# Three 256-token output projections recast as seven products of quarters, with tokens on the output partitions

## The chip, the cores and the metric

The kernel runs on one core of one Trainium2 chip. A core has a matrix engine (TensorE, PE in the profile), a vector engine (VectorE, DVE), a scalar engine (ScalarE, ACT), GpSimd (POOL), and DMA queues, here mostly issued from SyncE (SP). All arithmetic is 32-bit floating point. The metric is the device time of one launch, in microseconds (us); lower is better.

## The reference, cut to what matters

The reference runs a two-stream block of depth 2 and then a second block of depth 2, model width 1024. In every mixer the attention-like parts are concatenated into 1024 features per token, multiplied by a 1024x1024 output matrix, normalised over the features of a token and added to the residual stream:

```python
D_MODEL = 1024; SEQ = 256; NORM_EPS = 1e-6
def rms_norm(x, g):
    y = x * lax.rsqrt(jnp.mean(x * x, -1, keepdims=True) + NORM_EPS)
    return y * g
# first block, layer 1 (the "odd" mixer), latent tokens only:
y_lat = jnp.concatenate([c_lat.reshape(b, s_len, -1), d_lat.reshape(b, s_len, -1)], -1) @ w_out
# second block, for both layers (the "sparse" mixer):
mix = jnp.concatenate([y_attn, y_conv, y_pool], axis=-1)
mix = jnp.einsum('bse,ed->bsd', mix, w_out[i])
h = h + rmsnorm(mix, norm_mix_post[i])
m = rmsnorm(h, norm_mlp_pre[i])
m = jnp.square(jax.nn.relu(jnp.einsum('bsd,df->bsf', m, w_up[i])))
```

These are three products of 256 tokens x 1024 by 1024 x 1024: one in the odd mixer, one in each of the two sparse mixers. A fourth output projection, of the even mixer, has 512 tokens and is not part of the change.

## The kernel before, in words

Activations are kept with features on the 128 partitions: a tensor of 1024 features is eight tiles (k = 0 to 7) of 128 partitions by 256 or 512 tokens. `h` ("residual" in the profile) is the residual stream, `u` ("normed") the normalised input of a product, `y` ("branch") a product's output. The mixer's output lies in `R.mixed` (in "arena") for the odd mixer and in `R.mix2` ("mix") for the sparse ones.

Weights are read as 128x128 blocks, 16 to a chunk of 1 MB. SyncE loads all chunks in the order of use into a ring of five slots ("weight_ring"); a slot is loaded again when the last product that uses its chunk is done (`K.next_blocks` records which).

The program is a list of stages. Each stage adds a piece of program for each engine, and every engine runs its pieces strictly in the order of the stages (`K.add`); semaphores with counted values order the engines against each other. There is no scheduler. `K.in_turn` makes each vector instruction wait for the one before it where they depend on each other.

Around each of the three projections the stages are:

- `attention_stage` (L709): scores, softmax, transposed probabilities (L763), weighted values (L784). Its last instruction is on VectorE, L840, which writes the last part of the mixer's output. What the other mixers' parts wrote is there earlier.
- `matmul_stage` (L355, product at L396) with `squares=True`: for each of eight output tiles m, eight matmuls, with a weight block as the stationary operand and 128x256 activations as the moving one, into one of four banks of PSUM. ScalarE copies each result to `y` and squares it (L384); VectorE adds up the squares (L378). `root_table` (L530) loads ScalarE's table for the square root ahead of it.
- `residual` (L565) with `token_norm` (L497): the sum over the partitions by a matmul with ones (L513), root (L508), reciprocal (L522), and the spreading of the token's factor over partitions by a matmul (L517); then for each tile two instructions on VectorE, `y*gain*factor` (L575) and `h + y` (L581).
- `modulated_norm` (L535) with `scale_stage` (L446): ScalarE squares each tile of `h` as it is ready (L464), with two buffers for the squares; TensorE sums them by matmuls with ones (L482), eight accumulated in one bank; then the root (L469), a reciprocal of 128x256 (L490) and a scaling per tile (L546), of which the next product starts with the first tile. In the odd stage ScalarE also adds a shift (L558).
- the first product of the feed-forward part: L892 after the odd mixer, L396 from "normed" after the sparse ones.

`WideFeedForward` (L914), an older part of the kernel for 512 tokens, already uses seven products of quarters; its vector instructions on weights (L951 to L954) have the size of those that the change adds.

## Time and profile before

| | us |
|---|---|
| median of 3 runs | 2405.7 |
| lowest, highest | 2405.43, 2406.46 |
| the profiled execution, its own time | 2402.14 |
| its span, from the first to the last instruction | 2400.3 |
| TensorE busy in the span | 2271.0 (95%) |
| VectorE, ScalarE, GpSimd busy | 814.5, 462.9, 104.1 |
| granted TensorE clock, mean | 0.971 of full speed |

The page of the profile says which share of the span each engine is busy, which chain of instructions ended last, and which groups of instructions cost most. In rows of a group "L396 PE MATMUL out<-in 128*128 128x256 f32 x1504 | 325.6, 379" the figures behind the bar are the busy time of the group in us and the mean duration of one instruction in ns. One matmul of 32-bit data appears as two records of TensorE, and matmuls are pipelined: the mean duration of one is longer than the distance from one to the next, so a run's cost is its busy time over its records. PEld is the load of the stationary operand, which overlaps the matmuls. The granted clock is given as a share of full speed: 1.00 is 2.4 GHz, 0.50 is 1.2 GHz.

### The profile page before, as it was taken

The page shows a single profiled execution, that of the slowest core. Times are in us where ns is not written, and L with a number is a line of the kernel's source. Part 1 is how long each engine was busy: PE and PEld are TensorE (multiplying, and loading weights), DVE is VectorE, ACT ScalarE, POOL GpSimd, SP SyncE. Part 2 cuts the span into 40 slices and gives each one's busy share as a digit, 9 for nine tenths or more (in the row PEclk, how much of TensorE's full clock was granted, in tenths as well). Part 3 has the DMA queues.
Part 4 walks back from the last instruction along what each step waited for, and adds up shares of the span by engine and source line. Part 5 has one row for each costly group of instructions (what it writes and reads, how often), then busy time and mean ns, then how long its engine had stood idle before and what let it go on. Part 6 is the DMA issues. An engine that isn't in the chain of part 4 may idle for free.

```text
span 2400.3 us, 34069 instructions
## 1 busy us (share of the span) xinstructions
PE 2271.0 (95%) x15078; PEld 1713.8 (71%) x15078; DVE 814.5 (34%) x1541; ACT 462.9 (19%) x999; POOL 104.1 (4%) x126
## 2 busy tenths in 40 slices
PE   6999999998999999979999999988999999889998
PEld 3447877453888864454678888876888878678887
DVE  1565545643544440032331001763110138421002
ACT  2433221442100000020431000133110012311001
POOL 0003332001100000000000000000000000000000
PEclk8999999999999999989999999999999999899999
DMA  7221444205422222121123444322343333134332
GB/s 309 70 70 57 162 158 163 94 19 185 130 89 86 85 76 70 70 84 57 53 71 123 158 140 158 114 88 71 129 152 140 143 131 113 66 111 157 123 146 99
DMA packets 39074, 271.30 MB, mean 113 GB/s; under 512 B 4752, under 2 KB 6160, under 8 KB 6928
## 3 DMA queue, kind: packets, MB, share of 16 engines
q1 hardware_dynamic: 36752, 261.11, 30.6%
q0 software_dynamic: 1312, 3.15, 0.7%
q10 hardware_dynamic: 864, 4.87, 0.5%
q8 instruction: 119, 1.95, 0.3%
q14 instruction: 27, 0.22, 0.0%
HBM read 267.54 MB, written 1.05 MB: 112 GB/s over the span
## 4 chain that ended last, share of the span: by engine, by line
PE 87%; DVE 8%; ACT 3%; DMA 1%; issue 1%; ACTq 0%; DVEq 0%
PE banks L396 39%; PE banks L980 11%; PE banks L892 6%; PE banks L1472 5%; PE banks L2119 4%; PE banks L1155 2%; PE banks L1179 2%; PE banks L434 2%; PE banks L608 1%; PE banks L748 1%; PE banks L1175 1%; DVE arena L2271 1%; PE banks L482 1%; PE banks L763 1%; PE banks L754 1%
## 5 line engine op out<-in xcount | busy, mean ns | idle before, releaser
L396 PE MATMUL banks<-arena,weight_ring 128*128 128x256 f32 (+1 forms) x1856 | 476.8, 420 | 1.7 <-ACT arena L2534 0.9
L396 PEld LDWEIGHTS banks<-arena,weight_ring 128*128 128x128 f32 x1856 | 352.4, 190 | 125.2 <-issue 83.5
L396 PE MATMUL banks<-normed,weight_ring 128*128 128x256 f32 (+1 forms) x1296 | 305.3, 399 | 12.9 <-DVE normed L546 11.8
L396 PEld LDWEIGHTS banks<-normed,weight_ring 128*128 128x128 f32 x1296 | 250.0, 193 | 68.5 <-issue 19.1
L378 DVE TENSOR_TENSOR roots<-roots,squares 128x256 f32<-128x256 f32 (+1 forms) x56 | 27.6, 492 | 555.6 <-ACT squares L384 555.6
L892 PE MATMUL banks<-normed,weight_ring 128*128 128x256 f32 x704 | 152.2, 379 | 3.4 <-ACT normed L558 3.4
L2119 PE MATMUL banks<-normed,weight_ring 128*128 128x256 f32 x640 | 147.3, 391 | 5.9 <-DVE normed L546 5.9
L892 PEld LDWEIGHTS banks<-normed,weight_ring 128*128 128x128 f32 x704 | 133.6, 190 | 22.0 <-ACT normed L558 3.8
L2119 PEld LDWEIGHTS banks<-normed,weight_ring 128*128 128x128 f32 x640 | 125.1, 196 | 25.9 <-issue 4.7
L1472 PE MATMUL banks<-normed,weight_ring 128*128 128x512 f32 x288 | 126.1, 593 | 0.0
L396 PE MATMUL banks<-mix,weight_ring 128*128 128x256 f32 (+1 forms) x384 | 111.0, 451 | 3.0 <-DVE mix L840 1.6
L1472 PEld LDWEIGHTS banks<-normed,weight_ring 128*128 128x128 f32 x288 | 54.3, 190 | 66.7 <-issue 66.7
L396 PEld LDWEIGHTS banks<-mix,weight_ring 128*128 128x128 f32 x384 | 72.7, 190 | 40.4 <-issue 30.1
L2540 DVE TENSOR_TENSOR arena<-arena 128x256 f32<-128x256 f32 x64 | 27.2, 425 | 195.2 <-ACT arena L2534 195.2
L980 PE MATMUL banks<-normed,weight_ring 128*128 128x256 f32 x352 | 83.2, 391 | 7.1 <-ACT normed L558 4.9
L980 PEld LDWEIGHTS banks<-normed,weight_ring 128*128 128x128 f32 x352 | 68.9, 196 | 18.7 <-issue 5.8
L822 DVE TENSOR_REDUCE attention_small<-banks 128x1 f32<-128x512 f32 (+2 forms) x96 | 48.3, 531 | 66.1 <-PE banks L754 61.4
L608 PE MATMUL banks<-weight_ring,silu_cond 128*32 128x512 f32 x384 | 54.4, 652 | 15.5 <-ACT silu_cond L2431 7.1
L802 ACT ACTIVATE arena<-banks,attention_small 128x512 f32<-128x512 f32 (+2 forms) x96 | 54.0, 563 | 61.7 <-DVE attention_small L822 61.6
L2534 ACT ACTIVATE arena<-banks 128x256 f32<-128x256 f32 x64 | 24.6, 384 | 207.1 <-PE banks L396 207.1
L396 PE MATMUL banks<-residual,weight_ring 128*128 128x256 f32 x256 | 60.5, 402 | 2.6 <-DVE residual L581 2.6
L1326 POOL TENSOR_TENSOR mix<-arena,constants 128x512 f32<-128x512 f32 x48 | 56.4, 1201 | 125.4 <-DVE arena L1357 88.0
(372 smaller groups left out, 2713.3 us busy)
## 6 DMA issues: line engine op xcount, KB each, us to landing
weight_ring<-in_weights SPq DMA_DIRECT2D x248, 1024.0 KB, 4.9
constants<-in_const ACTq DMA_DIRECT2D x1, 2209.5 KB, 12.7
residual<-in_tokens ACTq DMA_DIRECT2D x1, 2048.0 KB, 12.7
mix<-in_rpb POOLq DMA_DIRECT2D x32, 64.0 KB, 8.5
out<-residual SPq DMA_DIRECT2D x1, 1024.0 KB, 4.8
branch<-arena POOLq DMA_DIRECT2D x1, 512.0 KB, 4.9
normed<-in_ple POOLq DMA_DIRECT2D x1, 512.0 KB, 3.7
vector_params<-in_vectors ACTq DMA_DIRECT2D x1, 223.0 KB, 5.8
```

The lines of the kernel that those rows point to most:

```text
L396: mm = pe.matmul(K.psum[lo:hi, banks[m % nb], 0:T], K.block(first[m] + k)[:, lo:hi], rhs(k), start=(k == 0), stop=(k == n_k - 1))
L434: mm = pe.matmul(K.bank(banks[t], width), lhs(k, t), K.block(first + k * n, n)[:, 0:width], start=(k == 0), stop=(k == n_k - 1))
L608: mm = pe.matmul(o, self.silu[:, k, :], self.K.block(self.first[k] + 4 * j, 4), start=(k == 0), stop=(k == KT - 1))
L802: act.activation(prob[:, i % 4, 0:x.n], K.bank(i % 4, x.n), ACT.Exp, bias=maximum[:, i % 4:i % 4 + 1], accum_out=total[:, i % 4:i % 4 + 1] ...
L822: dve.reduce_max(maximum[:, i % 4:i % 4 + 1], K.bank(i % 4, rounds[r].n), AX, negate=True).then_inc(sg["maxima"].sem, 1)
L892: mm = pe.matmul(K.bank(i % 4, T), K.block(first[i] + k), u[:, k, 0:T], start=(k == 0), stop=(k == KT - 1))
L980: mm = pe.matmul(self.outs(p)[i], a[:, k * P:k * P + P], right(k), start=(k == 0), stop=(k == H - 1))
L1155: mm = pe.matmul(heads(2 * u)[halves[n], m, :], L[u][lv % 2][halves[n], m, :], X[u][halves[n], m, :], start=True, stop=True)
L1179: mm = pe.matmul(heads(2 * u + 1)[halves[n], m, :], PR[u][halves[n], m, :], Y[u][halves[n], m, :], start=True, stop=True)
L1326: pool.tensor_tensor(out=L[u][lv % 2], in0=C[u], in1=bc(level[:, 6 * d + lv, :], 1, 8), op=ALU.mult).then_inc(sg["g_level"].sem, 1)
L1472: mm = pe.matmul(K.bank(f % 4), K.block(first[f] + k), u[:, k, :], start=(k == 0), stop=(k == KT - 1))
L2119: mm = pe.matmul(K.bank(m % 2, S), K.block(first[m] + k), u[:, k, 0:S], start=(k == 0), stop=(k == KT - 1))
```

## The change

The three projections leave `matmul_stage`, `residual` and their norm; a class `TokenProjection` takes their place. The operands swap sides: 128x128 tiles of the mixer's output become the stationary operand, and 512 output columns of weights the moving one, so that results have tokens on the partitions. The matrices are cut into quarters: the tokens in two halves, the 1024 output columns in two halves, and the 1024 inner features in even and odd tiles, taken as four pairs. For each of the four pairs seven products (128x128 by 128x512) are accumulated in seven banks. Products 1 and 2 use the raw operands; product 3 uses a raw weight quarter and a sum of tokens, product 4 a raw token quarter and a sum of weights, product 7 a difference of both. The sums are made on VectorE: four of 128x512 for the weights of each pair, and four over the tokens for each of two groups of pairs. At the end the seven results are combined into the four quarters of the output by seven additions.

Since a token now lies on a partition, its sum of squares comes from ScalarE's accumulator along the free axis; the four quarters are then scaled per partition, turned back to features on partitions by 16 transposes of 128x128, and added to `h` with the gain by one VectorE instruction per tile, which reads the transposed tile from PSUM. The weights are laid out row by row, aligned to chunks (1.25 chunks of zeros more in all), and in the sparse mixers the convolution's and pool's features now come first in `mix`. Products 1 and 2 of the first pairs (three pairs in the odd mixer, two in the sparse ones) don't wait for the end of attention.

```diff
+class TokenProjection:
+    BANK = {1: 4, 2: 5, 3: 6, 4: 7, 5: 0, 6: 1, 7: 2}
+    TURNED = (5, 6, 7, 3)
+    LAST = (1, 2, 6, 7, 5, 4, 3)
+    def __init__(self, K, x, n_k, token_sums, weight_sums, y, k_ready, groups, ahead=1):
+        self.K, self.n, self.k_ready, self.groups = K, n_k // 2, k_ready, groups
+        self.t, self.y, self.ahead = weight_sums, y, ahead
+        a = x.rearrange("p (i j) (c n) -> p i j c n", j=2, c=2)
+        self.a11, self.a12, self.a21, self.a22 = (a[:, :, j, c] for c in range(2) for j in range(2))
+        self.s1, self.s2, self.s4 = token_sums
+        n = self.n
...
+        for p in range(n):
+            K.next_blocks(CB, (self.sg["f_products"], self.at["f_products"] + (p + 1 if p < n - 2 else n + 5)))
...
+    def add_weights(self, dve, p):
+        K, sg, at = self.K, self.sg, self.at
...
+        if p >= 2:
+            dve.wait_ge(sg["f_products"].sem, at["f_products"] + p - 1)
+        step = K.in_turn(dve, "vector")
+        b11, b12, b21, b22 = (self.weights(p, r, i) for r in range(2) for i in range(2))
+        t1, t2, t3, t4 = self.t[p % 2]
+        dve.tensor_tensor(out=t3, in0=b22, in1=b12, op=ALU.subtract)
+        step(dve.tensor_tensor(out=t1, in0=b12, in1=b11, op=ALU.subtract))
+        step(dve.tensor_tensor(out=t2, in0=b22, in1=t1, op=ALU.subtract))
+        dve.tensor_tensor(out=t4, in0=b21, in1=t2, op=ALU.subtract).then_inc(sg["f_weights"].sem, 1)
+    def add_tokens(self, dve, g):
+        lo, hi = self.groups[g]
+        need(dve, self.k_ready(2 * hi - 1))
+        step = self.K.in_turn(dve, "vector")
...
+        step(dve.tensor_tensor(out=s1, in0=a21, in1=a22, op=ALU.add))
+        step(dve.tensor_tensor(out=a21, in0=a11, in1=a21, op=ALU.subtract))
+        step(dve.tensor_tensor(out=s2, in0=s1, in1=a11, op=ALU.subtract))
+        dve.tensor_tensor(out=s4, in0=a12, in1=s2, op=ALU.subtract).then_inc(self.sg["f_tokens"].sem, 1)
+    def run(self, h, gain, banks_free):
+        K, sg, at, n, y = self.K, self.sg, self.at, self.n, self.y
+        bank = {i: K.bank(b) for i, b in self.BANK.items()}
...
+        def final(i):
+            return (sg["f_products"], at["f_products"] + n - 2 + self.LAST.index(i) + 1)
+        def tensor(pe):
+            def product(p, i):
+                if p == 0 and i == 3:
+                    need(pe, banks_free)
+                left = {1: self.a11, 2: self.a12, 3: self.s4, 4: self.a22, 5: self.s1, 6: self.s2, 7: self.a21}[i]
+                right = {1: (0, 0), 2: (1, 0), 3: (1, 1)}.get(i)
+                if i in (1, 2, 4):
+                    need(pe, self.k_ready(2 * p + (i != 1)))
+                else:
+                    pe.wait_ge(sg["f_tokens"].sem, at["f_tokens"] + [lo <= p < hi for lo, hi in self.groups].index(True) + 1)
+                if right:
+                    K.arrived(pe, self.begin + CB * p)
+                    b = self.weights(p, *right)
+                else:
+                    pe.wait_ge(sg["f_weights"].sem, at["f_weights"] + p + 1)
+                    b = self.t[p % 2][{5: 0, 6: 1, 7: 2, 4: 3}[i]]
+                return pe.matmul(bank[i], left[:, p], b, start=(p == 0), stop=(p == n - 1))
+            ahead = self.ahead
+            for p in range(ahead):
+                for i in (1, 2):
+                    product(p, i)
+            for p in range(n - 2):
+                for i in range(1 if p >= ahead else 3, 8):
+                    mm = product(p, i)
+                mm.then_inc(sg["f_products"].sem, 1)
+            for i in self.LAST:
+                if i > 2 or n - 2 >= ahead:
+                    product(n - 2, i)
+                product(n - 1, i).then_inc(sg["f_products"].sem, 1)
+            def turn(q, k, half):
+                return pe.transpose(tile(k)[:, half * P:half * P + P], y[:, q, k % 4 * P:k % 4 * P + P], K.c("ident"))
+            for half in (1, 0):
+                done = 1 if half else 2
+                pe.wait_ge(sg["taken_out_by_vector"].sem, at["taken_out_by_vector"] + done)
+                for k in range(KT):
+                    if k == 4:
+                        pe.wait_ge(sg["taken_out_by_scalar"].sem, at["taken_out_by_scalar"] + done)
+                    mm = turn(2 * half + k // 4, k, half)
+                    if not half:
+                        mm.then_inc(sg["turned"].sem, 1)
+        def scalar(act):
+            need(act, [final(1)])
+            act.activation(y[:, 0], bank[1], ACT.Copy).then_inc(sg["f_first"].sem, 1)
+            for j, q in enumerate((0, 3, 2, 1)):
+                act.wait_ge(sg["f_quarters"].sem, at["f_quarters"] + j + 1)
+                if j == 2:
+                    act.wait_ge(sg["squared"].sem, at["squared"] + 1)
+                act.activation(K.square[:, j % 2], y[:, q], ACT.Square, accum_out=sums[:, q:q + 1]).then_inc(sg["squared"].sem, 1)
+                if j >= 2:
+                    half = 3 - j
+                    act.wait_ge(sg["summed"].sem, at["summed"] + 1)
+                    act.wait_ge(sg["squared"].sem, at["squared"] + j + 1)
+                    act.activation(root[:, half:half + 1], sums[:, q:q + 1], ACT.Sqrt, bias=partial[:, half:half + 1], scale=1.0 / D).then_inc(sg["rooted"].sem, 1)
+            for j, q in enumerate((3, 1)):
+                half = q // 2
+                act.wait_ge(sg["inverted"].sem, at["inverted"] + j + 1)
+                act.activation(y[:, q], y[:, q], ACT.Copy, scale=inverse[:, half:half + 1]).then_inc(sg["taken_out_by_scalar"].sem, 1)
+        def vector(dve):
+            step = K.in_turn(dve, "vector")
+            for p in range(2, n):
+                self.add_weights(dve, p)
+            add = lambda q, x, i: dve.tensor_tensor(out=y[:, q], in0=y[:, x], in1=bank[i], op=ALU.add)
+            dve.wait_ge(sg["f_first"].sem, at["f_first"] + 1)
+            need(dve, [final(6)])
+            step(add(1, 0, 6))
+            add(0, 0, 2).then_inc(sg["f_quarters"].sem, 1)
+            need(dve, [final(7)])
+            step(add(2, 1, 7))
+            need(dve, [final(5)])
+            step(add(1, 1, 5))
+            add(3, 2, 5).then_inc(sg["f_quarters"].sem, 1)
+            need(dve, [final(4)])
+            add(2, 2, 4).then_inc(sg["f_quarters"].sem, 1)
+            dve.wait_ge(sg["squared"].sem, at["squared"] + 2)
+            dve.tensor_scalar(partial, sums[:, 0:4:3], 1.0 / D, EPS, ALU.mult, ALU.add).then_inc(sg["summed"].sem, 1)
+            need(dve, [final(3)])
+            add(1, 1, 3).then_inc(sg["f_quarters"].sem, 1)
+            for half in (1, 0):
+                iv = inverse[:, half:half + 1]
+                dve.wait_ge(sg["rooted"].sem, at["rooted"] + 2 - half)
+                dve.reciprocal(iv, root[:, half:half + 1]).then_inc(sg["inverted"].sem, 1)
+                dve.wait_ge(sg["inverted"].sem, at["inverted"] + 2 - half)
+                dve.tensor_scalar(y[:, 2 * half], y[:, 2 * half], iv, None, ALU.mult).then_inc(sg["taken_out_by_vector"].sem, 1)
+            for k in range(KT):
+                dve.wait_ge(sg["turned"].sem, at["turned"] + k // 2 * 2 + 2)
+                dve.scalar_tensor_tensor(out=h[:, k, S:], in0=tile(k), scalar=gain(k, 1), in1=h[:, k, S:], op0=ALU.mult, op1=ALU.add).then_inc(sg["applied"].sem, 1)
+        K.add(tensor=tensor, scalar=scalar, vector=vector)
+        return [(sg["applied"], at["applied"] + KT)], lambda k: [(sg["applied"], at["applied"] + k + 1)]
...
-    return attention_stage(K, rounds, [mix[:, 0:4, t * P:t * P + P] for t in range(2)], ready, buf)
+    return attention_stage(K, rounds, [mix[:, 4:8, t * P:t * P + P] for t in range(2)], ready, buf)
...
+        def out_projection(mix, groups, n_early, gain, r):
+            K.next_blocks(-K.taken % CB, r[0])
+            fa = Area(R.arena[:, 0:10820])
+            weight_sums, token_sums = [[fa.get(512) for _ in range(4)] for _ in range(2)], [fa.get(4, P) for _ in range(3)]
+            to = TokenProjection(K, mix, KT, token_sums, weight_sums, token_y, lambda k: [] if k < 2 * n_early else r, groups, n_early)
+            def sums(dve):
+                need(dve, r)
+                to.add_weights(dve, 0)
+                to.add_tokens(dve, 0)
+                to.add_tokens(dve, 1)
+                to.add_weights(dve, 1)
+            K.add(vector=sums)
+            root_table(K)
+            return to.run(h, gain, r)
...
-                r = matmul_stage(K, KT, KT, lambda k: R.mixed[:, k, :], S, lambda e, m, ps: e.activation(y[:, m, 0:S], ps, ACT.Copy), r, squares=True)
-                r, tiles = residual(K, h, S, S, y, gain(1, 1), r)
+                r, tiles = out_projection(R.mixed, [(0, 3), (3, 4)], 3, gain(1, 1), r)
...
-            r = matmul_stage(K, KT, KT, lambda k: R.mix2[:, k, :], S, lambda e, m, ps: e.activation(y2[:, m, :], ps, ACT.Copy), r, squares=True)
-            r, tiles = residual(K, h, S, S, y2, plain("norm_mix_post"), r)
+            r, tiles = out_projection(R.mix2, [(0, 2), (2, 4)], 2, plain("norm_mix_post"), r)
```

TensorE, from the last instructions of the odd mixer's attention (L784 weighs the values; from "branch" are values, "arena" the probabilities) to the next product; before:

```order
L772 MATMUL banks<-constants,attention_small 64x128 x2
L784 MATMUL banks<-branch,arena 64x128 x16
L396 MATMUL banks<-arena,weight_ring 128x256 x64
L513 MATMUL banks<-constants,roots 128x1 x2
L517 MATMUL banks<-constants,token_roots 128x128 x2
L482 MATMUL banks<-squares,constants 128x256 x8
L892 MATMUL banks<-normed,weight_ring 128x256 x352
```

and of the change (its lines are two further on there; L961 is a product of `TokenProjection`, L977 a transpose, "weight_ring" as the moving operand a raw weight quarter, "arena" alone a sum of weights):

```order
L774 MATMUL banks<-constants,attention_small 64x128 x2
L786 MATMUL banks<-branch,arena 64x128 x16
L961 MATMUL banks<-weight_ring,arena 128x512 x7
L961 MATMUL banks<-arena 128x512 x4
L961 MATMUL banks<-weight_ring,arena 128x512
L961 MATMUL banks<-arena 128x512 x4
L961 MATMUL banks<-weight_ring,arena 128x512 x2
L961 MATMUL banks<-arena 128x512 x8
L961 MATMUL banks<-weight_ring,arena 128x512 x2
L977 MATMUL banks<-constants,branch 128x128 x16
L484 MATMUL banks<-squares,constants 128x256 x8
L1058 MATMUL banks<-normed,weight_ring 128x256 x352
```

The first seven raw products (six early ones and product 3 of pair 0) stand right behind attention, and 16 transposes stand where the matmuls with ones (L513) and for the spreading (L517) stood. The sums of squares (L482, now L484) and the next product are as before.

VectorE, from the last instruction of the odd mixer's attention (L840, now L842); before:

```order
L840 TENSOR_TENSOR arena<-banks,arena 128x512
L378 TENSOR_TENSOR roots<-roots,squares 128x256 x7
L522 RECIPROCAL token_roots<-token_roots 128x2
L575 SCALAR_TENSOR_TENSOR branch<-branch,gains,banks 128x256 x2
L581 TENSOR_TENSOR residual<-residual,branch 128x256
```

and of the change, up to the first addition of the results (L1011), where `add_weights` is L918 to L921 and `add_tokens` L929 to L932:

```order
L842 TENSOR_TENSOR arena<-banks,arena 128x512
L918 TENSOR_TENSOR arena<-weight_ring 128x512
L919 TENSOR_TENSOR arena<-weight_ring 128x512
L920 TENSOR_TENSOR arena<-weight_ring,arena 128x512
L921 TENSOR_TENSOR arena<-weight_ring,arena 128x512
L929 TENSOR_TENSOR arena<-arena 128x384
L930 TENSOR_TENSOR arena<-arena 128x3x128
L931 TENSOR_TENSOR arena<-arena 128x384
L932 TENSOR_TENSOR arena<-arena 128x384
L929 TENSOR_TENSOR arena<-arena 128x128
```

Sixteen instructions on sums (pair 0, both groups of tokens, pair 1) now follow the end of attention at once, of them eight ahead of product 3 of pair 0; those of pairs 2 and 3 follow and wait for products.

## Rows read from the trace of the kernel before

**Rows 1.** The page: engines; the chain that ended last, shares of the span.

```profile
PE 2271.0 (95%) x15078; PEld 1713.8 (71%) x15078; DVE 814.5 (34%) x1541; ACT 462.9 (19%) x999; POOL 104.1 (4%) x126
...
PE 87%; DVE 8%; ACT 3%; DMA 1%; issue 1%; ACTq 0%; DVEq 0%
```

**Rows 2.** Windows over the three stages: length, busy and count per engine, clock, DMA.

```profile
1220.10:1263.72 43.62, 35.68 (x154) 28.93 (x153) 12.57 (x29) 10.30 (x30) 0.00 (x0) 0.92 0.29 97
1635.89:1679.20 43.31, 35.96 (x152) 29.02 (x152) 12.04 (x28) 10.59 (x28) 0.00 (x0) 0.91 0.29 98
2085.38:2127.89 42.51, 35.21 (x152) 28.60 (x152) 12.03 (x28) 10.59 (x28) 0.00 (x0) 0.96 0.29 100
sum 129.44, PE 106.86 PEld 86.55 DVE 36.64 ACT 31.47 POOL 0.00; mean PE 35.62 PEld 28.85 DVE 12.21 ACT 10.49 POOL 0.00
```

**Rows 3.** Timeline, odd mixer, end of attention: start, us, instruction, [idle before].

```profile
1218.18 1.92 PE L784 MATMUL banks<-branch,arena 128*64 128x128 f32 x32
...
1220.15 0.69 DVE L840 TENSOR_TENSOR arena<-banks,arena 128x512 f32<-128x512 f32 x1 [1.43 <-PE banks L784]
...
1220.89 27.89 PE L396 MATMUL banks<-arena,weight_ring 128*128 128x256 f32 x128 [0.79 <-DVE arena L840]
```

**Rows 4.** Groups by form, TensorE: L396, 512 and 256 moving columns.

```profile
L396 PE MATMUL banks<-arena,weight_ring 128*128 128x512 f32 x352 | 151.2, 592 | 0.0
...
L396 PE MATMUL banks<-mix,weight_ring 128*128 128x256 f32 x256 | 55.8, 380 | 1.6 <-DVE mix L840 1.6
```

**Rows 5.** Groups by form, VectorE: sums of 256 and 512 columns; a 512-column scaling.

```profile
L378 DVE TENSOR_TENSOR roots<-roots,squares 128x256 f32<-128x256 f32 x42 | 17.9, 426 | 369.1 <-ACT squares L384 369.1
...
L954 DVE TENSOR_TENSOR arena<-weight_ring,arena 128x512 f32<-128x512 f32 x11 | 7.6, 692 | 0.4
...
L1628 DVE TENSOR_SCALAR arena<-arena,vector_params 128x512 f32<-128x512 f32 x12 | 5.8, 483 | 25.4 <-ACT arena L1550 25.4
```

**Rows 6.** Timeline, odd mixer, from the projection's end to the next product's norm.

```profile
1249.52 0.42 DVE L378 TENSOR_TENSOR roots<-roots,squares 128x256 f32<-128x256 f32 x1 [3.03 <-ACT squares L384]
...
1251.21 0.86 PE L517 MATMUL banks<-constants,token_roots 128*128 128x128 f32 x4 [0.55 <-DVE token_roots L522]
...
1252.11 0.87 DVE L575 SCALAR_TENSOR_TENSOR branch<-branch,gains,banks 128x256 f32<-128x256 f32 x2 [0.95 <-PE banks L517]
...
1253.35 0.42 ACT L464 ACTIVATE squares<-residual 128x256 f32<-128x256 f32 x1 [2.39 <-DVE residual L581]
...
1253.82 6.49 PE L482 MATMUL banks<-squares,constants 128*128 128x256 f32 x16 [1.75 <-ACT squares L464]
...
1260.34 0.47 ACT L469 ACTIVATE roots<-banks,constants 128x256 f32<-128x256 f32 x1 [0.79 <-PE banks L482]
```

**Rows 7.** Timeline, second sparse mixer: ScalarE squares while the clock is full.

```profile
2123.32 0.96 ACT L464 ACTIVATE squares<-residual 128x256 f32<-128x256 f32 x2 [0.31 <-PE banks L482]
```

**Rows 8.** Timeline, attention of the odd mixer: four transposes, eight records.

```profile
1210.64 1.09 PE L763 MATMUL banks<-constants,arena 128*128 128x128 f32 x8
```

**Rows 9.** Groups by form, ScalarE: a 512-column square; reading the accumulator.

```profile
L464 ACT ACTIVATE squares<-residual 128x512 f32<-128x512 f32 x16 | 10.1, 631 | 18.1 <-DVE residual L581 13.1 <-PE banks L482 4.9
...
L802 ACT ACTIVATION_READ_ACCUMULATOR arena<-banks,attention_small 128x1 f32 x96 | 19.3, 201 | 0.0
```

**Rows 10.** Windows: squares' sums in the sparse mixers; first 6.4 us of feed-forward products.

```profile
1669.45:1676.32 6.87, 6.77 (x16) 3.74 (x16) 4.20 (x12) 2.92 (x7) 0.00 (x0) 0.60 0.00 0
2118.95:2125.03 6.08, 6.02 (x16) 3.31 (x16) 4.19 (x12) 2.92 (x7) 0.00 (x0) 0.75 0.00 1
1263.72:1270.12 6.40, 6.40 (x30) 5.58 (x31) 4.89 (x14) 3.96 (x9) 0.00 (x0) 1.00 0.00 0
1679.20:1685.60 6.40, 6.40 (x16) 5.18 (x17) 2.72 (x7) 0.00 (x0) 0.00 (x0) 0.54 0.00 0
2127.89:2134.29 6.40, 6.40 (x22) 5.26 (x23) 3.15 (x8) 0.38 (x1) 0.00 (x0) 0.73 0.00 0
```

**Rows 11.** The page: the ring's DMA issues, KB each, us to landing.

```profile
weight_ring<-in_weights SPq DMA_DIRECT2D x248, 1024.0 KB, 4.9
```

32 lines of the change are left out of this document (25 added, 7 removed).

## The prediction

> **What bounds the kernel now.** I read first the engines' busy times and the chain that ended last: TensorE is busy for 95% of the span and holds 87% of that chain, VectorE 8%, ScalarE 3% [rows 1]. So a removed column of matmul work is worth its time, and so is a shorter chain of VectorE and ScalarE wherever TensorE waits for it. Next the three stretches that the change rewrites, from the end of attention's last matmul to the first matmul of the feed-forward part: 43.62, 43.31 and 42.51 us, together 129.44 us, 5.4% of the span, in which TensorE is busy 106.86 us and the DMA engines 0.29 of the time [rows 2]. Nothing else in the program is changed but the ring's alignment. Then the timeline of the odd mixer. Attention's matmuls end at 1218.18 + 1.92 = 1220.10; VectorE's L840 ends 0.74 us later, and the products start 0.79 us after TensorE went idle and run 27.89 us, to 1248.78 [rows 3]. From there to the next product it is 14.94 us: 4.57 us until ScalarE squares the first finished tile of the residual (1253.35), 6.99 us of squares and their sums until the root can start (1260.34), and 3.38 us of root, reciprocal and first scaled tile, to 1263.72 [rows 2, 6]. TensorE idles or works in bits there. The sparse mixers have the same parts; with the same 0.78 us and 27.89 us ahead, their tails are 14.64 and 13.84 us.
>
> **The products.** Before, 64 matmuls of 256 columns. The form costs 55.8 us for 256 records, 0.218 us each, two records a matmul [rows 4]: 64 x 2 x 0.218 = 27.9 us, which is the row of the timeline. Now 28 matmuls (seven products by four pairs) of 512 columns. That form costs 151.2 us for 352 records, 0.430 us each [rows 4]: 28 x 2 x 0.430 = 24.1 us. The columns fall by an eighth and the time with them: 3.8 us less. The stationary loads halve in number and stay hidden. The first products no longer wait for VectorE's L840: 0.79 us earlier.
>
> **The wait that is added at the start.** Product 3 of pair 0 needs the sums of tokens, and behind it on TensorE stands everything else. VectorE starts on sums when attention's L840 is done, at +0.74 us after TensorE's last attention matmul. Four sums of 512 columns cost 4 x 0.69 = 2.8 us, and four of the first token group come behind them: 384 columns in the odd mixer, between 0.43 (256 columns) and 0.69 us (512) [rows 5], I take 0.56, so 2.2 us; in the sparse ones 256 columns, 4 x 0.43 = 1.7 us. Tokens are ready at +5.8 and +5.3 us with a little for the semaphores. TensorE has raw products for six or four times 0.86 us, to +5.2 and +3.4 us. It waits 0.7 us in the odd mixer and 1.9 us in a sparse one. The later sums (2.8 us a pair) are made beside the 4.3 us that the five remaining products of a pair take; only pair 3's sums in the odd mixer can be late, since two of its products were spent early: pair 1 ends, 2.8 us of sums against three products of 0.86 us, 0.3 us. With roundings I take 1.1 us and 2.0 us. Bounds: no wait at all if semaphores and the 384 columns are cheap, and 3 us a stage if VectorE runs a third slower beside TensorE's wider reads. The nearest rows are the same instructions in the older seven-product stage, which run beside matmuls at 0.69 us, so I stay with them.
>
> **The tail after the last product (E).** Six of the seven results are combined and three quarters of the output squared while products still run. On the path stand: the last addition (0.69) to E+0.75; ScalarE's square of that quarter with the accumulator's reading, 0.63 + 0.20 [rows 9], to E+1.55, its root, reciprocal on VectorE and a scaling of 512 columns (0.48 on VectorE [rows 5], 0.63 on ScalarE), to about E+2.7 and E+3.2. The other half of the tokens is scaled earlier (E+1.5), so TensorE begins to transpose there. Four transposes took 1.09 us alone, in a stream some 0.87 [rows 8]: first half in two groups from E+1.55 to E+3.4, second half from E+3.4 to E+5.1. After its first two tiles (E+3.9) VectorE adds tile 0 to the residual, one instruction of 0.47, and the first square starts at E+4.45. Before it was E+4.57: this part is worth nothing by itself. What it takes out (L513, the token root, L522, L517, L575) is replaced link for link.
>
> What follows, the squares and their sums, is unchanged code, but its pace is not fixed. ScalarE and TensorE hand two buffers back and forth; in the second sparse mixer, once the clock is full, a pair of tiles takes 0.96 us of ScalarE plus 0.31 us of waiting, 0.64 us a tile [rows 7]. At half clock TensorE's share doubles: eight tiles take 6.87 us at a mean clock of 0.60 and 6.08 at 0.75 [rows 10], against 8 x 0.64 = 5.1 at full clock. In all three stages the clock falls after TensorE has had only 1.4 us of work in the 5 us behind the products. In the changed kernel TensorE has 16 transposes, 3.5 us, in the same stretch. If the clock holds, the sums start behind the transposes at E+5.15 and end at E+10.2; from their end to the next product it is 2.88 and 2.86 us in the sparse mixers (1676.32 and 2125.03 to the stages' ends) and 3.41 in the odd one, with its shift [rows 2, 6, 10], so the next product comes at E+13.05, in the odd mixer at E+13.55. If it doesn't, 7 x 0.23 = 1.6 us more.
>
> The Trainium skill, "TensorE: Matmul & The Clock Gate", section "Part 4: PE-mode transpose", says that transposes don't count as activity for the clock as matmuls do. In attention a third of the records are transposes and the clock stays full, which doesn't separate them; by the rule the lower pace would come back, and the last rival below is its case.
>
> **Sum**, from attention's last matmul to the next product, clock full: odd 24.1 + 1.1 + 13.55 = 38.75, less 43.62 = -4.9. Sparse 24.1 + 2.0 + 13.05 = 39.15: -4.15 and -3.35. Together -12.4 us; with the slow pace in all three, -12.4 + 4.8 = -7.6. I take the middle, -10. The alignment adds 1.25 chunks to 248 and moves loads; a load lands in 4.9 us [rows 11], a chunk feeds 6.9 us of products, and three chunks are released before E, so it costs nothing; without that cover a late chunk would cost up to 4.9 us once. After the start of the feed-forward part the clock matters again: over its first 6.4 us it was 1.00, 0.54 and 0.73 [rows 10], so 0, 3.0 and 1.7 us were lost. I expect the same sum in other places, with some 3 us of spread, as all later waits shift too.
>
> The profiled execution took 2402.1 us, with 1.8 us outside its span; the median of the runs is 3.6 us above it. The difference of -10.2 goes on the median: 2405.7 - 10.2 = 2395.5 us.
>
> **Rivals.**
> - *The tail stays slow.* Clock down through the squares in all stages and 1 us lost to links that I timed too short: -7.6 + 3 x 0.6 = -5.8, 2400 us. For it: the fall in all three stages of before. Against it: 3.5 us of new TensorE work in that stretch.
> - *VectorE becomes the bound.* Its work during the products is 16 x 0.69 + 8 sums of tokens (3.5) + 7 x 0.69 = 19.4 us of 24. If each is a third longer, 26 us, the products wait: 3 x 2.5 us lost, -3 us, 2403 us. Rows 5 show no such stretching.
> - *The clock also holds at the start of the feed-forward parts*: -12.4 and 3 of the 4.7 us lost there come back, 2391 us. For it: busier tails. Against: TensorE still idles 2.9 to 3.4 us for root and reciprocal before that start.
> - *Slower: transposes at half clock.* The mechanism: if transposing doesn't hold the clock, it falls around E+1.5; the 16 transposes then take 3.5 us more, of which 2.5 lie on the path, the eight sums take 8 x 0.86 = 6.9 us instead of 5.1 and start behind the transposes, so the root comes 5.2 us later than in my sum, in all three stages +15.6; the feed-forward parts begin at half clock too, 3 x 3.0 against 4.7 us now: +4.3. -12.4 + 19.9 = +7.5, 2413 us. It decides if more than 12 of these 20 us come. Against it: matmuls for the sums follow the transposes at once, and in before the clock recovered during them. The Trainium skill's "TensorE: Matmul & The Clock Gate", "Part 4: PE-mode transpose", speaks for this case.
> - *It doesn't do what it says* would be 512-column matmuls with activations as the stationary operand at another rate than [rows 4]; the form is the same to TensorE, and I give it nothing of its own.
>
> **Chances.** Forecast (-8 to -12.4) 0.57, slow tail (-4.8 to -8) 0.21, clock better (below -12.4) 0.11, VectorE or several small losses (within 0.2%) 0.08, slower 0.03. What a measurement can tell from no change is 0.2%, 4.8 us. Faster 0.89, same 0.08, slower 0.03. The range: from -15.5, with the clock's gain and its spread, to -4.5, where the slow tail ends: 2390.2 to 2401.2.
>
> **What would show it.** Right: L961 at 0.430 us a record and 56 records; a wait of TensorE for VectorE's L932 of about 0.7 us (odd) and 1.9 us (sparse), none for L921 but a short one; the first L466 4.4 us after the last product; the stages at 38.8 and 39.2 us, and 40.4 and 40.8 where the clock fell. Wrong: waits for L921 in the middle of the products (VectorE bound), a granted clock of 0.50 during L977, a wait for the weight ring, or a stage of over 42 us.

## The result, and the profile after

The changed kernel takes 2383.97 us (median of 4 runs, 2383.33 to 2390.61) where the kernel before took 2405.56 us in the same session (4 runs, 2402.86 to 2406.46): ratio 0.9918, 95% interval 0.9899 to 0.9938. The forecast was 2395.5 us, 2390.2 to 2401.2: faster was right, by too little, and the time lies below the range. A repetition in another session (`whole_again`, below) gave a smaller gain, 0.9939 [0.9924, 0.9954], which is 14.9 us by the medians; the two intervals overlap. As a difference the range reached to -15.5 us, so the second session lies just inside it and the first, at -21.6, far outside; in both the forecast of -10.2 was too small.

The page after the change; first the engines, then the chain's shares (answers to [rows 1]):

```profile
PE 2256.5 (95%) x14886; PEld 1670.5 (70%) x14886; DVE 856.5 (36%) x1601; ACT 462.1 (19%) x987; POOL 103.8 (4%) x126
...
PE 86%; DVE 9%; ACT 3%; DMA 1%; issue 1%; ACTq 0%; DVEq 0%
```

TensorE has 14.5 us less to do and VectorE 42 us more. The windows over the three rewritten stages, columns as in [rows 2]:

```profile
1216.69:1255.16 38.47, 31.42 (x89) 14.46 (x89) 26.68 (x49) 10.05 (x26) 0.00 (x0) 1.00 0.31 109
1628.83:1668.35 39.52, 32.64 (x88) 16.04 (x88) 26.15 (x48) 10.34 (x24) 0.00 (x0) 0.95 0.38 133
2070.24:2108.97 38.73, 31.18 (x90) 14.63 (x89) 26.15 (x48) 10.23 (x24) 0.00 (x0) 0.99 0.38 136
sum 116.72, PE 95.25 PEld 45.12 DVE 78.98 ACT 30.61 POOL 0.00; mean PE 31.75 PEld 15.04 DVE 26.33 ACT 10.21 POOL 0.00
```

129.44 us became 116.72: 12.72 less, against 12.4 in my sum with the clock full. The profiled executions differ by 17.6 us in span (2400.3 and 2382.7), so 4.9 us are outside the stages, in code that the change doesn't touch: -3.4 ahead of the odd mixer's stage (1216.69 against 1220.10), +1.5 from there to the first sparse one, -4.3 between the two sparse ones, +1.3 at the end. Behind the first stage that is -1.5 net. Another 4.0 us of the 21.6 come from which executions were profiled: the one of before took 3.4 us less than its median.

The timeline of the start, odd mixer (answers to [rows 3]):

```profile
1214.77 1.92 PE L786 MATMUL banks<-branch,arena 128*64 128x128 f32 x32
...
1216.62 5.42 PE L961 MATMUL banks<-weight_ring,arena 128*128 128x512 f32 x12
...
1221.89 0.56 DVE L932 TENSOR_TENSOR arena<-arena 128x384 f32<-128x384 f32 x1
...
1222.60 1.10 PE L961 MATMUL banks<-weight_ring,arena 128*128 128x512 f32 x2 [0.56 <-DVE arena L932]
...
1223.53 3.60 PE L961 MATMUL banks<-arena 128*128 128x512 f32 x8
...
1226.97 1.02 PE L961 MATMUL banks<-weight_ring,arena 128*128 128x512 f32 x2
```

The first products follow attention without a gap, and the wait for the last sum of tokens is 0.56 us. In each sparse mixer it is 1.74 us. From 1223.53 to 1226.97 eight records begin, one each 0.430 us. The tail of the same mixer (answers to [rows 6]); the last product ends at about 1242.38:

```profile
1242.42 0.69 DVE L1011 TENSOR_TENSOR branch<-branch,banks 128x512 f32<-128x512 f32 x1 [0.95 <-PE banks L961]
...
1243.76 0.66 PE L977 MATMUL banks<-constants,branch 128*128 128x128 f32 x4 [1.38 <-DVE branch L1032]
...
1244.92 1.53 PE L977 MATMUL banks<-constants,branch 128*128 128x128 f32 x12 [0.50 <-ACT branch L1005]
1245.83 3.22 DVE L1035 SCALAR_TENSOR_TENSOR residual<-banks,gains,residual 128x256 f32<-128x256 f32 x8 [0.86 <-PE banks L977]
1246.35 0.81 ACT L466 ACTIVATE squares<-residual 128x256 f32<-128x256 f32 x2 [0.87 <-DVE residual L1035]
...
1246.81 4.93 PE L484 MATMUL banks<-squares,constants 128*128 128x256 f32 x16 [0.37 <-ACT squares L466]
...
1251.78 0.47 ACT L471 ACTIVATE roots<-banks,constants 128x256 f32<-128x256 f32 x1 [0.79 <-PE banks L484]
...
1255.16 1.22 PE L1058 MATMUL banks<-normed,weight_ring 128*128 128x256 f32 x2 [3.42 <-ACT normed L560]
```

All sixteen transposes are sixteen records, 2.19 us together. The sums of the eight tiles' squares take 4.93 us (6.49 before). The tail, from the last product to the next one, is 12.78 us instead of 14.94: 0.6 us less to the first square (3.97 against 4.57), 1.56 less from there to the root (5.43 against 6.99), and the last part as before (3.38). The same rows of the first sparse mixer, in which the clock fell to half speed (1.2 GHz) for 3.4 us just as the second group of transposes began, 10.7 us ahead of the stage's end:

```profile
1657.57 2.81 PE L977 MATMUL banks<-constants,branch 128*128 128x128 f32 x12 [0.50 <-ACT branch L1005]
1660.18 5.30 PE L484 MATMUL banks<-squares,constants 128*128 128x256 f32 x16
1668.35 1.22 PE L398 MATMUL banks<-normed,weight_ring 128*128 128x256 f32 x2 [2.87 <-DVE normed L548]
```

A window over that stretch, with its granted clock of 0.50:

```profile
1657.62:1661.00 3.38, 3.38 (x14) 3.14 (x15) 1.87 (x6) 1.32 (x3) 0.00 (x0) 0.50 1.01 422
```

That is 1.28 us more for twelve transposes and 0.37 more for the sums. Groups by form of the products and the transposes (x, busy, mean ns; [rows 4, 8]), and the page's row of the ring ([rows 11]):

```profile
L961 PE MATMUL banks<-arena 128*128 128x512 f32 x64 | 29.5, 593 | 0.4 <-DVE arena L921 0.4
...
L977 PE MATMUL banks<-constants,branch 128*128 128x128 f32 x48 | 7.8, 316 | 5.6 <-DVE branch L1032 4.1 <-ACT branch L1005 1.5
```

```profile
weight_ring<-in_weights SPq DMA_DIRECT2D x249, 1024.0 KB, 5.0
```

Outside the stages the granted clock tells the parts apart. Windows over the part between the two sparse stages, in the kernel before and in the one after:

```profile
1679.20:2085.38 406.18, 389.25 (x1872) 332.61 (x1872) 121.64 (x301) 61.67 (x158) 0.45 (x6) 0.96 0.35 125
```

```profile
1668.35:2070.24 401.89, 385.02 (x1873) 329.31 (x1873) 121.48 (x301) 61.66 (x158) 0.45 (x6) 0.98 0.36 126
```

The instructions are the same; TensorE is busy 4.23 us less, at a clock of 0.98 instead of 0.96. By the trace's records of the clock it stood at half speed for 33.2 us of this part before, and for 20.0 us after: in five stretches, at places in the part that differ by 3 us at most, of which four are 3.4 us shorter after the change (of the first a piece lies ahead of the part).

### The profile page after: what moved, and what is told of

Read it like the earlier page. It is cut to its first block, busy times and chain, and to the rows that moved or that the text cites. A ratio compares the mean times of both kernels' runs of the same rounds, so it can differ in the third digit from the quotient of the medians.

```text
span 2382.7 us, 33833 instructions
## 1 busy us (share of the span) xinstructions
PE 2256.5 (95%) x14886; PEld 1670.5 (70%) x14886; DVE 856.5 (36%) x1601; ACT 462.1 (19%) x987; POOL 103.8 (4%) x126
## 4 chain that ended last, share of the span: by engine, by line
PE 86%; DVE 9%; ACT 3%; DMA 1%; issue 1%; ACTq 0%; DVEq 0%
PE banks L398 36%; PE banks L1146 11%; PE banks L1058 6%; PE banks L1638 5%; PE banks L2285 4%; PE banks L961 2%; PE banks L1321 2%; PE banks L1345 2%; PE banks L436 1%; PE banks L610 1%; PE banks L750 1%; PE banks L1341 1%; DVE arena L2437 1%; PE banks L765 1%; PE banks L786 1%
## 5 line engine op out<-in xcount | busy, mean ns | idle before, releaser
L398 PE MATMUL banks<-arena,weight_ring 128*128 128x256 f32 (+1 forms) x1728 | 448.9, 423 | 0.9 <-ACT arena L2716 0.9
L398 PEld LDWEIGHTS banks<-arena,weight_ring 128*128 128x128 f32 x1728 | 328.2, 190 | 121.0 <-issue 83.5
L398 PE MATMUL banks<-normed,weight_ring 128*128 128x256 f32 (+1 forms) x1296 | 305.5, 399 | 12.8 <-DVE normed L548 11.8
L380 DVE TENSOR_TENSOR roots<-roots,squares 128x256 f32<-128x256 f32 (+1 forms) x35 | 18.6, 532 | 477.2 <-ACT squares L386 477.2
L2285 PEld LDWEIGHTS banks<-normed,weight_ring 128*128 128x128 f32 x640 | 125.0, 197 | 25.7 <-issue 4.6
L2722 DVE TENSOR_TENSOR arena<-arena 128x256 f32<-128x256 f32 x64 | 27.2, 425 | 195.1 <-ACT arena L2716 195.1
L610 PE MATMUL banks<-weight_ring,silu_cond 128*32 128x512 f32 x384 | 54.4, 651 | 15.6 <-ACT silu_cond L2597 7.2
L1197 DVE TENSOR_TENSOR arena<-squares,banks 128x512 f32<-128x512 f32 x22 | 15.1, 687 | 137.5 <-ACT squares L1174 137.5
L1072 DVE TENSOR_TENSOR arena<-banks,arena 128x256 f32<-128x256 f32 x22 | 9.3, 424 | 139.8 <-PE banks L1058 135.5
## 6 DMA issues: line engine op xcount, KB each, us to landing
residual<-in_tokens ACTq DMA_DIRECT2D x1, 2048.0 KB, 12.8
```

Source lines behind the costliest of these rows:

```text
L398: mm = pe.matmul(K.psum[lo:hi, banks[m % nb], 0:T], K.block(first[m] + k)[:, lo:hi], rhs(k), start=(k == 0), stop=(k == n_k - 1))
L610: mm = pe.matmul(o, self.silu[:, k, :], self.K.block(self.first[k] + 4 * j, 4), start=(k == 0), stop=(k == KT - 1))
L2285: mm = pe.matmul(K.bank(m % 2, S), K.block(first[m] + k), u[:, k, 0:S], start=(k == 0), stop=(k == KT - 1))
```

## The experiments

Three sessions on three chips, each with the kernel before beside it. Differences between kernels of different sessions go by their ratios to it.

### The change again, and its halves

Theory A: the stages are worth what their timelines say, and the rest of the gain is where the clock's slow stretches fall. Rival: something that the change does outside its stages, as the ring's new alignment. `whole_again` is the changed kernel itself:

> The changed kernel once more, against before in five rounds. Theory A (three stages): the two profiles give 12.7 us less in the three changed stages and 4.9 us less elsewhere, all of the latter in stretches where the granted clock was 0.50 in one and 1.00 in the other; if that part were mere luck of two executions, the medians should come to 12 to 15 us apart (ratio 0.994 to 0.995). Rival B (shifted waits): the later waits fall differently against the clock in every execution, so the medians stay 17 to 22 us apart (0.991 to 0.993), and the profile again shows fewer stretches at half clock after 1260 us than the 73 us of before.

Measured: 2388.63 us (5 runs, 2382.6 to 2391.34), before 2403.51 (17 runs, 2396.36 to 2406.23), ratio 0.9939 [0.9924, 0.9954]. Stages 38.46, 39.54 and 38.71 us: the same to 0.02. Ahead of the first stage 1214.62. The two parts between the stages:

```profile
1253.08:1629.75 376.67, 361.64 (x1745) 309.42 (x1745) 112.69 (x282) 59.92 (x150) 1.03 (x7) 0.96 0.36 125
1669.29:2071.26 401.97, 385.07 (x1873) 329.34 (x1873) 121.54 (x301) 61.67 (x158) 0.45 (x6) 0.98 0.36 126
```

The medians are as far apart as theory A said. Its profile is mixed: the part between the sparse stages is short again (401.97), but the part ahead of them takes 4.5 us more than in the profile of before (372.17). Behind the first stage, outside the stages, this kernel gained nothing on before (+1.6 us). The stages repeat to hundredths, the whole kernel doesn't.

`only_odd` keeps the old projection and its packing in the sparse mixers:

```
-            r, tiles = out_projection(R.mix2, [(0, 2), (2, 4)], 2, plain("norm_mix_post"), r)
+            r = matmul_stage(K, KT, KT, lambda k: R.mix2[:, k, :], S, ... squares=True)
+            r, tiles = residual(K, h, S, S, y2, plain("norm_mix_post"), r)
```

> The change in the odd mixer alone. Theory A: its stage from 43.6 to 38.5 us, so -5.2 us, ratio 0.998. Rival B: anything between -10 and 0, since all that follows is shifted by 5 us against the clock; its stage alone still 38.5.

Measured: 2398.43 us (11 runs), ratio 0.9982 [0.9970, 0.9993], -4.3 us by the ratio. Stages 38.47, 43.33, 42.65.

`only_sparse` is the other half: the old odd mixer, by the like edit there.

> The change in the two sparse mixers alone. Theory A: -3.8 and -3.8 us, together -7.6, ratio 0.997. Rival B: -2 to -15, with stages of 39.5 and 38.7 us (plus or minus 0.8 by the clock) all the same.

Measured: 2390.93 us (5 runs), ratio 0.9949 [0.9936, 0.9961], -12.3 us (-15.4 to -9.4). Stages 43.63, 39.53, 38.44. The two halves sum to -16.6 us. By their stages the odd half should bring 5.0 us and does; the sparse half should bring 7.8 us and brings 12.3. Its windows between the sparse stages, `only_odd` first, then `only_sparse`:

```profile
1675.15:2081.33 406.18, 389.25 (x1872) 332.55 (x1872) 121.64 (x301) 61.69 (x158) 0.45 (x6) 0.96 0.35 125
```

```profile
1677.12:2079.08 401.96, 385.07 (x1873) 329.31 (x1873) 121.54 (x301) 61.66 (x158) 0.45 (x6) 0.98 0.36 126
```

The part is 4.2 us shorter where the sparse stage is the new one, and as before where it isn't. So in these kernels the 4.2 us come with the new sparse stage, though none of its code runs there. The part between the odd and the first sparse stage shows no such order: `only_sparse` runs the code of before up to the end of that part, and took 375.36 us there against 372.17. In that part two executions of the same code differ by 3 us.

### What of the gain is the seven products: `eight_raw`

The same layout and tail with eight raw products of quarters, no sums of weights or tokens. The core of the edit, in place of the seven products and their sums:

```
+            for p in range(n - 2):
+                for q in range(4):
+                    mm = product(p, q)
+                mm.then_inc(sg["f_products"].sem, 1)
+            for q in self.LAST:
+                product(n - 2, q)
+                product(n - 1, q).then_inc(sg["f_products"].sem, 1)
```

> Tokens on partitions, norm along the free axis, transposes and tail as in the change, but eight raw products of quarters a pair (32 matmuls of 512 columns) in place of seven; no sums and no additions of results. Theory (the seven products are worth 3.45 us of matmuls a stage, less what their sums make TensorE wait: 1.0, 1.7, 1.7 us, and less one addition of 0.7 us behind the last product): stages of 27.6 + 12.1 (+0.3 odd) = 39.7 to 40.0 us against 38.5, 39.5 and 38.7, so 2 to 3 us slower in sum than the change and some 10 faster than before in the stages. Rival (the gain is the seven products'): about 43 us a stage, no faster than before.

Measured: 2387.8 us (6 runs, 2380.53 to 2394.67), ratio 0.9936 [0.9918, 0.9954]. Stages 39.65, 39.10, 39.38, together 118.13 us. VectorE is busy 8.2 to 8.8 us a stage instead of 26. Eight products cost 1.4 us more in the three stages than seven, where I expected 2 to 3 (2.5 us where the clock is full in both, `eight_fill` against `fill` below), and nothing that the medians can tell. So 11.3 of the 12.7 us come with the layout: no wait at the start (0.8 us a stage) and a shorter tail. A part of it is the clock's: the three stages stood at half clock for 17.9 us before and for 1.5 us here, and at the price found below (0.31 to 0.43 us for each us) that is 5 to 7 us, an estimate. Seven products save 8 x 0.43 = 3.4 us a stage over eight; the waits for sums (0.98 and 1.74 us) and the last addition (0.69) take 1.7 and 2.4 us of that. With the clock full in both, 1.2 us (odd) and 0.7 us (sparse) are left, 0.6 and 0.3 us less than this sum leaves; what takes those isn't shown.

### VectorE's order: `sums_order`

```
-                to.add_weights(dve, 0)
                 to.add_tokens(dve, 0)
-                to.add_tokens(dve, 1)
+                to.add_weights(dve, 0)
                 to.add_weights(dve, 1)
+                to.add_tokens(dve, 1)
```

and on TensorE product 3 of both first pairs comes ahead of their products of sums.

> The changed kernel with VectorE making both pairs' first sums of tokens ahead of the sums of weights of pair 1, and TensorE doing the raw product 3 of both pairs before the five summed products. Theory A (TensorE's order and the waits set the stages; what lies outside them is the clock's): the wait for L932 falls from 0.56 to 0.2-0.4 us in the odd mixer and from 1.74 to 0.2-0.4 us in each sparse one, the three stages go from 116.7 to 113.0-113.6 us in sum, the median is 3 us below the changed kernel's in the same session (ratio to before 0.992-0.993). Rival (the wait only moves to the sums of weights, L921, which now come later): the stages stay at 116.0-116.7 us and the median is the changed kernel's, 0.994.

Measured: 2385.46 us (5 runs; before 2403.73, 11 runs), ratio 0.9924 [0.9912, 0.9936]. The timeline of the first sparse mixer's start:

```profile
1629.44 3.70 PE L961 MATMUL banks<-weight_ring,mix 128*128 128x512 f32 x8
...
1631.65 0.42 DVE L932 TENSOR_TENSOR arena<-mix,arena 128x256 f32<-128x256 f32 x1
...
1632.98 1.88 PE L961 MATMUL banks<-weight_ring,arena 128*128 128x512 f32 x4
```

The wait of 1.74 us is gone: the sums are ready 0.9 us before TensorE wants them. Windows over its stages and the part between the sparse ones:

```profile
1217.06:1255.66 38.60, 32.89 (x88) 15.67 (x88) 26.68 (x49) 10.04 (x26) 0.00 (x0) 0.95 0.31 109
1629.51:1666.17 36.66, 31.15 (x89) 14.54 (x89) 26.05 (x48) 10.34 (x24) 0.00 (x0) 0.99 0.41 144
2072.22:2109.14 36.92, 31.13 (x88) 14.62 (x88) 26.05 (x48) 10.22 (x24) 0.00 (x0) 1.00 0.40 143
...
1666.17:2072.22 406.05, 389.16 (x1873) 332.64 (x1873) 121.64 (x301) 61.67 (x158) 0.45 (x6) 0.96 0.35 125
```

The stages fall by 4.5 us to 112.18, more than the 3.1 to 3.7 I had reckoned, although the odd one lost 0.9 us at half clock (37.68 in `sums_fill`, below); the first sparse one gained some 1.1 from a full clock. But the part between the sparse stages is back at 406.05 us and a clock of 0.96, as in the kernel before. So the 4.2 us outside aren't a property of the new projection, nor of the ring's alignment, which is the same here as in the changed kernel: they go with where the clock's stretches lie against the part's start. In the four kernels with 406.1 to 406.2 us (`before`, `only_odd`, `before_later_12`, `sums_order`) the first stretch at half clock begins 0.9 to 1.0 us ahead of that start and lasts 6.8 us; in the three with 401.9 to 402.0 (the changed kernel twice, `only_sparse`) it begins 0.4 to 0.5 us ahead and lasts 3.4 us. Within each group all five stretches have the same lengths, at the same places within 0.2 us. The median is 3.6 us lower than that of `whole_again` by the ratios, with intervals that overlap. Rival (the wait moves to L921): fallen.

### Work in the pre-norms' waits: `fill`, `before_fill`, `sums_fill`

If the clock is what is lost there, TensorE kept busy in the 2.9 us of root and reciprocal should bring it back. The edit, behind the sums of squares of each pre-norm:

```
+        for _ in range(fill):
+            pe.matmul(K.bank(5, P), K.c("ones"), K.c("ones"), start=True, stop=True)
```

with fill 10 at 256 tokens and 20 at more. Nothing reads these products.

> The changed kernel with 10 (256 tokens) or 20 (wider) more matmuls of ones, 128x128, behind the sums of squares of each pre-norm, so that TensorE isn't idle in the 2.9 us of root and reciprocal; they end before the next product may start. Theory A (the granted clock is what differs between the kernels outside the stages, and it falls behind these waits): the stretches at granted clock 0.50 that begin at the feed-forward starts go, half-clock time falls from about 118 to 70-95 us over the span, and the median is 5 to 15 us below the changed kernel's, with the stages proper as before (116.7 us) to +-1. Rival (the clock isn't held by such short work, or the lost time outside the stages isn't the clock's): half-clock time unchanged within 10 us, and the median within 3 us of the changed kernel's.

Measured: 2374.73 us (5 runs, 2372.22 to 2384.45), ratio 0.9886 [0.9870, 0.9902], 12.7 us under `whole_again` by the ratios, and 7.7 us under the changed kernel's first session. The first sparse mixer, and windows over the sparse stages and the part between them:

```profile
1661.58 2.39 PE L487 MATMUL banks<-constants 128*128 128x128 f32 x20
1664.62 1.56 PE L398 MATMUL banks<-normed,weight_ring 128*128 128x256 f32 x6 [0.64 <-DVE normed L550]
```

```profile
1626.18:1664.62 38.44, 33.42 (x109) 16.93 (x109) 26.15 (x48) 10.33 (x24) 0.00 (x0) 1.00 0.39 137
2062.69:2101.42 38.73, 33.41 (x109) 17.01 (x109) 26.15 (x48) 10.23 (x24) 0.00 (x0) 1.00 0.37 136
...
1664.62:2062.69 398.07, 384.43 (x1893) 330.44 (x1893) 121.33 (x301) 61.67 (x158) 0.45 (x6) 0.98 0.36 127
```

The filling lies wholly in the wait: the next product waits 0.64 us behind it. The stages are at full clock, half-clock time over the span falls from 114.1 to 76.3 us, and a kernel with more work is faster.

> The kernel before, with the same filling behind the sums of squares of each pre-norm. Theory A: the clock's share is the same kind of loss in both kernels, so this one gains too: 5 to 15 us against the kernel before, half-clock time down from about 138 us to 90-115, stages still 129 us less what the clock gives at their ends (at most 1). Rival: median within 3 us of the kernel before.

The same edit in the kernel before. Measured: 2393.15 us (6 runs), ratio 0.9958 [0.9944, 0.9972], -10.6 us by the medians, half-clock time from 138.3 to 93.9 us; the part between the sparse stages 399.45 us. The stages proper stay at 129.43. The loss to the clock is in both kernels, and between half and two thirds of what this change brings (21.6 and 14.9 us in the two sessions) are to be had there without it.

> Both edits together. Theory A: the gains add, stages 113.0-113.6 us, half-clock time 70-95 us, median 8 to 18 us below the changed kernel's. Rival: as sums_order alone, since the filling does nothing.

Measured: 2371.52 us (4 runs, 2369.03 to 2373.52), ratio 0.9863 [0.9849, 0.9877]. Stages 37.68, 36.67 and 36.94 us, 111.29 in sum where I expected 113.0 or more: 5.4 less than in the changed kernel, 1.1 of it the clock's. The two gains add, within the intervals.

### A shift, and the transposes' size: `before_later_12` and `turns_twice`

`before_later_12` shifts everything behind the odd mixer's attention in the kernel before, by twelve such matmuls ahead of its projection:

```
+                    for _ in range(12):
+                        pe.matmul(K.bank(5, P), K.c("ones"), K.c("ones"), start=True, stop=True)
```

> The kernel before with twelve more matmuls of ones, 128x128, ahead of the odd mixer's output projection: 2.6 us of work, and everything behind it later by that. Theory A (what is lost to the clock outside the stages depends on where its stretches fall against the waits, so a shift alone changes it): the parts between the rewritten stages change by 1 to 5 us in one of them, together with half-clock time there, and the median differs from +2.6 us by 1 us or more. Rival (a shift changes nothing outside): 2.6 +- 0.6 us more, parts between within 0.5 us of before's 372.2 and 406.2.

Measured: 2405.35 us (12 runs; before 2402.1, 17 runs), ratio 1.0012 [1.0002, 1.0022], which is +2.9 us, 0.5 to 5.3. The stage is 2.90 us longer, the part behind it 375.93 us instead of 372.17, with 8.8 us more at half clock, the next part 406.20, unchanged. The part changed as theory A said, but `only_sparse`, which has no shift, took 375.36 us there with the same code, so this doesn't show that the shift did it. The median is what the rival said, and its interval is too wide to tell. The experiment is inconclusive: no run here shows that a shift alone moves time.

`turns_twice` makes each transpose twice, as in my sum, which had taken them for two records each:

```
+                    turn(2 * half + k // 4, k, half)
                     mm = turn(2 * half + k // 4, k, half)
```

> The changed kernel with every transpose of the normed products made twice: 16 more transposes a stage. By the trace after the change one is a single record of 0.11-0.13 us, so 16 more are 1.8-2.0 us of TensorE, about half of it on the path. Theory A (the transposes were sized twice too long in my sum): this kernel is what I had summed for the changed one; each stage gets 0.4 to 1.2 us longer, 1.2 to 3.6 us in all. Rival (their cost is hidden behind ScalarE's squares, and the size didn't matter): the stages stay within 0.5 us in all.

Measured: 2388.77 us (6 runs), ratio 0.9945 [0.9931, 0.9959]. Its three stages:

```profile
1222.22:1261.36 39.14, 32.90 (x105) 16.19 (x104) 26.68 (x49) 10.05 (x26) 0.00 (x0) 1.00 0.30 107
1635.40:1674.51 39.11, 32.66 (x105) 16.27 (x105) 26.15 (x48) 10.34 (x24) 0.00 (x0) 1.00 0.38 135
2076.83:2116.22 39.39, 32.66 (x104) 16.36 (x105) 26.15 (x48) 10.23 (x24) 0.00 (x0) 1.00 0.37 134
```

0.67 us more in the odd stage and in the second sparse one, each at full clock on both sides; that is the size of the term. The first sparse stage is 0.4 us shorter, since here it kept the full clock: 39.11 against 38.44 in `fill`, also at full clock, is 0.67 again. In all the stages are 0.9 us longer, less than the 1.2 expected, and the median can't tell the two kernels apart.

### Toward a better kernel: `sums_fill_all`, `eight_fill`

`sums_fill_all` adds three such matmuls in the wait of each per-token norm of 256 tokens and six behind its spreading.

> The version with both edits (VectorE's sums in the new order, TensorE filled in the waits of the pre-norms), and in the norms that are taken per token and spread by TensorE (256 tokens) three more matmuls of ones, 128x128, while the root is taken and six behind the spreading. Theory A: half-clock stretches ahead of the mixers' starts shrink further, half-clock time from 86 to 60-80 us, median 1 to 6 us below that version's in the same session's terms (ratio to before 0.984-0.986). Rival: the added matmuls lie on the path (9 x 0.22 = 2.0 us a norm) and cost what they bring: 0.986-0.988.

Measured: 2367.32 us (5 runs, 2362.87 to 2375.49), ratio 0.9848 [0.9831, 0.9866]: the fastest kernel here, 34.8 us under the one before, though its lead over `sums_fill` is within the intervals. Half-clock time 68.3 us.

> The variant with eight raw products of quarters (no sums of weights or tokens) with the filling of the pre-norms. Theory A (seven products are worth no more than eight raw ones here: 118.1 against 116.7 us in the stages, and the new layout carries the gain): 1 to 2 us above the changed kernel with the filling, ratio to before 0.989-0.990. Rival (the eight raw products had a lucky clock): 4 us or more above it, 0.9905 or more.

Measured: 2374.34 us (4 runs), ratio 0.9882 [0.9865, 0.9899], the same as `fill`; the rival's 0.9905 or more lies outside. With the clock held the eight raw products are still no slower than the seven: in the stages 118.12 against 115.64 us, less than the medians can tell.

All profiles together, one of each kernel (us; "between 1" is from the odd to the first sparse stage, "between 2" from there to the second, "half" the time at half clock in that part, from the trace's records of the clock):

| kernel | three stages | ahead | between 1 (half) | between 2 (half) | end |
|---|---|---|---|---|---|
| before | 129.44 | 1220.10 | 372.17 (23.9) | 406.18 (33.2) | 272.4 |
| after | 116.72 | 1216.69 | 373.67 (27.0) | 401.89 (20.0) | 273.7 |
| whole_again | 116.71 | 1214.62 | 376.67 (33.5) | 401.97 (20.0) | 273.8 |
| only_odd | 124.45 | 1219.63 | 373.72 (27.0) | 406.18 (33.2) | 272.4 |
| only_sparse | 121.60 | 1218.60 | 375.36 (30.7) | 401.96 (20.0) | 271.3 |
| eight_raw | 118.13 | 1213.67 | 376.02 (32.8) | 403.81 (23.8) | 272.3 |
| sums_order | 112.18 | 1217.06 | 373.85 (27.2) | 406.05 (33.1) | 271.5 |
| fill | 115.64 | 1216.79 | 370.92 (20.5) | 398.07 (17.1) | 270.9 |
| sums_fill | 111.29 | 1217.68 | 368.39 (13.7) | 402.99 (27.3) | 270.8 |
| before_fill | 129.43 | 1220.08 | 371.84 (20.5) | 399.45 (17.1) | 270.2 |
| turns_twice | 117.64 | 1222.22 | 374.04 (27.3) | 402.32 (20.4) | 270.1 |
| before_later_12 | 132.36 | 1216.23 | 375.93 (32.7) | 406.20 (33.3) | 272.4 |
| eight_fill | 118.12 | 1214.99 | 371.84 (20.5) | 399.36 (17.1) | 270.7 |
| sums_fill_all | 111.98 | 1222.13 | 370.78 (13.7) | 398.90 (10.2) | 269.9 |

A line through the fourteen points of either part between gives 0.35 and 0.36 us of time for each us at half clock, with correlations of 0.97 and 0.95. Without the five kernels that have the filling it is 0.43 and 0.31, with 0.99 in both. That accounts for the 4.2 us: 13.2 us less at half clock in between 2, at 0.31, is 4.1.

## Why the prediction was right in the stages and wrong in the time

- **Products.** 0.430 us a record and 56 records a stage: as measured, 3.44 us for eight records in the timeline of the start. Right.
- **Waits at the start.** Foreseen 0.7 us (odd) and 1.9 (sparse); measured 0.56 and 1.74, with 0.42 for L921 in the odd one (foreseen 0.3). From the start to the last product's end it is 25.7 us in the odd mixer and 26.2 in the sparse ones, foreseen 25.2 and 26.1. Right.
- **Ahead of the squares.** The first L466 comes 3.97 us after the last product, foreseen 4.45. Here a term was mis-sized: "16 transposes, 3.5 us" is 2.19 us in the trace. I took the eight records of [rows 8] for four transposes, as its title says; they were eight (128 of the 540 records in attention's last 60 us are transposes, a quarter and not "a third"). With the second half done at E+4.1 instead of E+5.1, the sums start at E+4.4 instead of E+5.15, and the next product comes at E+12.8 (odd) and E+12.5 (second sparse) instead of 13.55 and 13.05. `turns_twice` shows the size: 0.67 us a stage, 2 us in all.
- **The clock in the tail.** "If the clock holds" was nearly the case: two tails at full clock but for 0.3 and 0.8 us, the first sparse one down for 3.4 us, which cost 1.1 us (39.52 against 38.44 in `fill`). "I take the middle, -10" priced the slow pace at half of 4.8 us and was too slow; the stages gave -12.7. With the transposes at their measured size the sum would have been -14.4 with the clock full, so errors cancelled in part in the -12.4 that looks so close: the clock's 1.1 us and 0.7 us more from the starts to the last products' ends went the other way. My sign "a granted clock of 0.50 during L977" did come in one stage of three, where the clock fell as the second group of transposes began, after waits of 1.38 and 0.50 us. But it cost 1.1 us there, not the 5.2 us of the rival *transposes at half clock*, and the time of 2413 us didn't come. That rival fell: in `turns_twice` with 32 transposes a stage all three tails are at 1.00. That speaks against the use I made of the rule in the Trainium skill, "TensorE: Matmul & The Clock Gate", "Part 4: PE-mode transpose"; it doesn't refute it, since matmuls of the sums follow at once.
- **Outside the stages.** "I expect the same sum in other places, with some 3 us of spread" is the step that failed, together with the choice of -10. By the medians the gain outside the stages was 21.6 - 12.7 = 8.9 us in the first session and 14.9 - 12.7 = 2.2 us in the second, where the sum had nothing and the range 3 us. Two things were missing.
- **What the clock does in unchanged code.** Between the sparse stages the changed kernel is 4.2 us faster in both of its profiles, and in `only_sparse`, and not in `only_odd` or `sums_order`. I had seen that a clock stretch at a stage's start costs us, and gave it three starts of 6.4 us (4.7 us in all); the trace of before has 138 us at half clock, 57.1 of them in the parts between. Such a stretch costs a third of its length. The end behind the last stage takes 1.3 us more in both profiles of the changed kernel, so that some 2.9 us repeat in all. With the stages' 12.7 that is 15.6 us, near the 14.9 of the second session. This is a sum of profiled parts; no experiment changed the clock between the sparse stages alone.
- **Scatter of the executions.** The rest of the first session's 21.6 us, some 6 us, goes with no code that changed: 3.4 us lie ahead of the first rewritten stage, and 4.0 us, less 1.5 that were lost between the odd and the first sparse stage, are the profiled executions' distance from the medians. The program ahead of that stage is the same in all fourteen kernels but for the filling, and took 1213.67 to 1222.22 us; the median of before stood on three runs within 1.0 us, and its 17 runs of the second session spread from 2396.36 to 2406.23. My range had no term for that. The half-clock time doesn't explain the part ahead (correlation 0.1, and 0.5 over the nine kernels without the filling), and what does stays open. That the second session fell inside the range is therefore partly luck, as is the size of the miss in the first.
- **Slips in the working.** -10 became -10.2 in the forecast without a reason, and the rival *the tail stays slow* speaks of 1 us lost to links but adds 3 x 0.6. Neither changes a verdict.
- **The clock at the start of the feed-forward parts** (a rival): it didn't hold. Over the first 6.4 us behind the stages it was 0.76, 0.77 and 0.53 after the change, where it had been 1.00, 0.54 and 0.73.
- **VectorE as the bound** (a rival): didn't come. It is busy 26 us a stage, 19.46 of them from the odd mixer's start to the last addition of the results, where I had summed 19.4; a 512-column sum takes 692 ns as before.
- **The ring's alignment** costs nothing: 249 loads, 5.0 us to landing, no wait of TensorE for the ring in the stages. A chunk feeds 24.1 / 4 = 6.0 us of products there, not the 6.9 that I wrote, which is the figure of before.

## What to carry to other kernels

Sum the part that a change rewrites by its timeline, and then count the stretches at half clock in what it doesn't rewrite: here 138 us of them cost about a third of their length (measured in the two parts between), and in one unchanged part what ran ahead of it decided over 4 us, as much as a good edit. Take both kernels in a second session before you credit a difference of some us to an edit: the same pair gave 21.6 and 14.9. Where TensorE waits 3 us for a root and a reciprocal, idle matmuls that end before the data is ready brought 0.4 to 0.5%, in the old kernel as in the new. And before seven products are used for eight, try eight in the same layout: the layout gave 11.3 of the 12.7 us in the stages.

## What the runs showed of the hardware

- A 128x128 fp32 transpose is one record, 0.13 us each in the run of twelve (1.53 us) and 0.11 by the difference to the run of four ((1.53 - 0.66) / 8), while an fp32 matmul is two: 0.430 us each for 512 columns, 0.218 for 256.
- Matmuls that nobody reads, in the pre-norms' waits (20 records, 2.39 us, at 256 tokens), cut half-clock time from 114 to 76 us and the kernel's time by 7.7 or 12.7 us, by the session compared with; in the kernel before, 10.6 us.
- Time at half clock costs 0.31 to 0.43 us per us in the parts between, not a half. TensorE is busy for 0.82 of those stretches in both parts before, and for 0.84 and 0.90 after; half of that would be 0.41 to 0.45, an estimate that fits the first part's 0.43 and lies above the second's 0.31. Why that one costs less isn't shown.
- The same instructions ahead of the first stage took 1214 to 1222 us in the profiles, while the three stages of the changed kernel repeated within 0.02 us in its two. Between kernels the same stage varies more, the second sparse one from 38.44 to 38.73 us.
